# One chain of squares per half, and attention heads placed between projection chunks

## The reference, cut to what matters

```python
# x: (16, 2048, 1024); 4 heads of 256; 256 memory tokens
x = x + merged @ w_out[l]                      # mixer's output projection
hq = rms_norm(x, xattn_norm_g[l])
q = (hq @ w_q[l]).reshape(b, s, 4, 256)
k, v = jnp.split(mem_n @ w_kv[l], 2, axis=-1)
pr = softmax(einsum("bshd,bmhd->bhsm", q, k) * 256 ** -0.5)
x = x + einsum("bhsm,bmhd->bshd", pr, v).reshape(b, s, d) @ w_o[l]
hf = rms_norm(x, ffn_norm_g[l])
...
x = x + (gelu(gate) * val) @ w_down[l]         # gated MLP
# rms_norm(x, g) = x * rsqrt(mean(x*x) + 1e-6) * g
```

## Time and profile before

| | |
|---|---|
| runs | 4116.72 us median of 3 (4114.6 to 4533.86) |
| profiled execution | 4116.1 us; span of its slowest core 4114.6 us, of the others 4102.6 to 4113.3 us |
| PE busy | 3876.9 us (94%), 18224 matmuls |
| DVE busy | 2683.5 us (65%) |
| ACT busy | 1953.7 us (47%) |
| POOL busy | 197.7 us (5%) |
| mean granted TensorE clock | 0.984 to 0.988 by core |
| chain that ended last | PE 81%, ACT 7%, DVE 6%, issue 3%, DMA 2% |

### The profile page before, as it was taken

How to read it: one execution, slowest core, us unless ns; L and a number is a source line. 1 busy time by engine, 2 the same in 40 slices (tenths; PEclk the granted TensorE clock), 3 DMA queues, 4 the chain that set the end, 5 groups by cost and what they waited for, 6 DMA issues and landing times.

```text
span 4114.6 us, 56669 instructions; the slowest of 8 cores (4102.6 to 4114.6 us)
## 1 busy us (share of the span) xinstructions
PE 3876.9 (94%) x18224; PEld 1784.1 (43%) x18224; DVE 2683.5 (65%) x3336; ACT 1953.7 (47%) x3779; POOL 197.7 (5%) x379
## 2 busy tenths in 40 slices
PE   6999999999998999999989999999999999999998
PEld 3444444444443445434444444543444434444343
DVE  4538775387754876649675387653867549665587
ACT  3445444464444544446443464434644346452544
POOL 1000000000000000000010000000000000000000
PEclk9999999999999999999999999999999999999999
DMA  6443352434842345323464424534346424352342
GB/s 138 117 82 68 65 107 58 82 68 80 168 103 51 59 78 110 62 49 67 106 136 103 84 56 81 99 64 84 65 108 136 103 49 73 68 106 52 57 75 70
DMA packets 108815, 348.19 MB, mean 85 GB/s; under 512 B 11888, under 2 KB 46960, under 8 KB 83952
## 3 DMA queue, kind: packets, MB, share of 16 engines
q0 software_dynamic: 41760, 275.11, 37.0%
q1 hardware_dynamic: 66768, 69.46, 5.7%
HBM read 586.05 MB, written 16.78 MB: 147 GB/s over the span
## 4 chain that ended last, share of the span: by engine, by line
PE 81%; ACT 7%; DVE 6%; issue 3%; DMA 2%; SPq 0%; DVEq 0%; ACTq 0%; POOLq 0%; POOL 0%
PE ps L424 81%; DVE X L401 2%; ACT SQ L397 2%; DVE H L411 2%; ACT F L397 2%; ACT AR L397 2%; DMA AR<-AR 1%; DVE SQ L401 1%; DVE X L411 1%; ACT RS L397 0%; DMA AR<-xT 0%; SPq L872 0%; ACT L397 0%; DVE F L411 0%; DMA RING<-wst 0%
## 5 line engine op out<-in xcount | busy, mean ns | idle before, releaser
L424 PE MATMUL ps<-H,RING 128*128 128x512 bf16 x10240 | 2265.0, 381 | 66.4 <-ACT GB L397 25.3
L424 PEld LDWEIGHTS ps<-H,RING 128*128 128x128 bf16 x10240 | 1004.2, 98 | 1286.6 <-issue 110.7
L424 PE MATMUL ps<-AR,RING 128*128 128x512 bf16 x4864 | 1096.7, 386 | 0.0
L397 ACT ACTIVATE AR<-ps 128x512 bf16<-128x512 f32 (+1 forms) x1024 | 598.5, 600 | 637.8 <-PE ps L424 610.8
L411 DVE SCALAR_TENSOR_TENSOR F<-AR,VEC,F 128x1024 f32<-128x1024 bf16 (+1 forms) x576 | 687.9, 1194 | 111.8 <-ACT F L397 69.1
L424 PEld LDWEIGHTS ps<-AR,RING 128*128 128x128 bf16 x4864 | 482.7, 99 | 590.2 <-issue 39.1
L397 ACT ACTIVATE SQ<-X 128x512 bf16<-128x512 f32 x384 | 240.2, 629 | 599.8 <-DVE X L401 561.9
L401 DVE TENSOR_TENSOR X<-ps,X 128x512 f32<-128x512 f32 x512 | 339.6, 684 | 200.3 <-PE ps L424 200.2
L397 ACT ACTIVATE GB<-ps 128x512 bf16<-128x512 f32 x320 | 183.1, 604 | 433.1 <-PE ps L424 431.5
L397 ACT ACTIVATE GB<-F 128x1024 bf16<-128x1024 f32 x192 | 189.3, 986 | 287.0 <-DVE F L411 286.4
L515 POOL DMA_DIRECT2D RING<-wst x280 | 147.8, 528 | 3598.7 <-PE ps L424 3578.4
(11 more groups left out here) (75 smaller groups left out, 1954.5 us busy)
## 6 DMA issues: line engine op xcount, KB each, us to landing
RING<-wst POOLq DMA_DIRECT2D x184, 1024.0 KB, 9.3
RING<-wst POOLq DMA_DIRECT2D x64, 704.0 KB, 7.8
RING<-wst POOLq DMA_DIRECT2D x32, 768.0 KB, 6.7
AR<-AR SPq DMA_DIRECT2D x256, 64.0 KB, 3.5
X<-xT SPq DMA_DIRECT2D x64, 256.0 KB, 12.8
yT<-X SPq DMA_DIRECT2D x64, 256.0 KB, 9.4
AR<-xT SPq DMA_DIRECT2D x40, 256.0 KB, 7.0
WX<-wst POOLq DMA_DIRECT2D x8, 1280.0 KB, 15.9
```

What stands on the lines that cost most here:

```text
L397: S.add("act", lambda h: h.activation(out=out.ap, in_=in_.ap, func=func, scale=s, **kw), reads=rd, writes=out.keys)
L424: S.add("pe", lambda h: h.matmul(out.ap, lhsT=lhsT.ap, rhs=rhs.ap, start=start, stop=stop), reads=lhsT.keys + rhs.keys, writes=out.keys)
```

## The change

`residual_stage` is split: `residual_items` gives the list of chunks, and the stage runs them as before. In it the squares of a half form one chain, with each addition issued one chunk after its square was, and one ONESK matmul after chunk 7. `proj_group` gives its inner loop to `run_items`. `attn` now projects Q for s = 0 first; then it runs heads 0 to 2 of s = 0, with Q chunks of s = 1 between a head's scores and its denominator; then head 3 of s = 0 and head 0 of s = 1 as a pair; then heads 1 to 3 of s = 1, with output chunks of s = 0 between. The output projection's `lead_group` is gone.

```diff
--- before.py
+++ after.py
@@ -647,14 +647,17 @@
                     flush()
                 if lead[s]:
                     lead_group(items[:lead[s]], s)
-                for blk, ncol, col0, rhs, evac in items[lead[s]:]:
-                    b_ = blk(s) if callable(blk) else blk
-                    nk = len(rhs)
-                    ps = P.next()
-                    for kc in range(nk):
-                        MM(ps.v(), b_.v(kc * ncol + col0, kc * ncol + col0 + 128), sub(rhs[kc], s), kc == 0, kc == nk - 1)
-                    evac(s, ps)
-                    tick()
+                run_items(items[lead[s]:], s)
+
+        def run_items(items, s):
+            for blk, ncol, col0, rhs, evac in items:
+                b_ = blk(s) if callable(blk) else blk
+                nk = len(rhs)
+                ps = P.next()
+                for kc in range(nk):
+                    MM(ps.v(), b_.v(kc * ncol + col0, kc * ncol + col0 + 128), sub(rhs[kc], s), kc == 0, kc == nk - 1)
+                evac(s, ps)
+                tick()
 
         def norm_stats_fin(s, pn):
             rs = RSB.v(s * ST, (s + 1) * ST)
@@ -673,33 +676,40 @@
                     reads=o.keys, dma_sem="out%d_%d" % (c, s))
                 out_tokens.append(tok)
 
-        def residual_stage(items_wo_evac, kind, gbase, lead):
+        def residual_items(items_wo_evac, kind, gbase):
             pn = [P.take(), P.take()]
             last = kind == "final"
             lag_apply = (3, 5) if last else (0, 0)
             b, hf = now["b"], now["hf"]
 
-            prev_sq = {}
+            sqs = [[], []]
 
             def mk(oc):
                 def ev(s, ps):
                     TT("dve", sub(X[oc], s), ps.v(), sub(X[oc], s), ALU.add)
                     sq = SQR.next()
                     ACT(sq.v(), sub(X[oc], s), AF.Square)
-                    if oc % 4:
-                        TT("dve", sq.v(), sq.v(), prev_sq[s].v(), ALU.add)
-                    prev_sq[s] = sq
+                    sqs[s].append(sq)
+
+                    def add():
+                        a, b_ = sqs[s].pop(0), sqs[s][0]
+                        TT("dve", b_.v(), b_.v(), a.v(), ALU.add)
+
+                    if oc >= 2:
+                        add()
                     tag = 2 if last else s
-                    if oc % 4 == 3:
-                        defer(lambda: MM(pn[s].v(), ONESK.v(), sq.v(), oc == 3, oc == 7), 3, tag)
                     if oc == 7:
+                        add()
+                        defer(lambda: MM(pn[s].v(), ONESK.v(), sq.v(), True, True), 3, tag)
                         defer(lambda: norm_stats_fin(s, pn), 3, tag)
                         for c in range(8):
                             defer(lambda c=c: norm_apply(s, c, kind, gbase, b, hf), 3 + lag_apply[s] + c // 2, tag)
                 return ev
 
-            items = [(blk, ncol, col0, rhs, mk(oc)) for oc, (blk, ncol, col0, rhs) in enumerate(items_wo_evac)]
-            proj_group(items, True, (lead, 0))
+            return [(blk, ncol, col0, rhs, mk(oc)) for oc, (blk, ncol, col0, rhs) in enumerate(items_wo_evac)]
+
+        def residual_stage(items_wo_evac, kind, gbase, lead):
+            proj_group(residual_items(items_wo_evac, kind, gbase), True, (lead, 0))
 
         def mem_load(b):
             for i_ in range(2):
@@ -975,33 +985,56 @@
                         ACT(VV[mc].v(jb * 512, (jb + 1) * 512), ps.v(), AF.Copy)
                         tick()
             wqb = [ring_get(l, "wq0"), ring_get(l, "wq1")]
-            proj_group([(wqb[qc // 4], 512, (qc % 4) * 128, H,
-                         (lambda s, ps, qc=qc: ACT(sub(Q[qc], s), ps.v(), AF.Identity, scale=1.0 / 16))) for qc in range(8)], True, (0, 4))
-            ri = 0
-            for hd in range(4):
-                for s in range(2):
-                    E = []
+            qi = [(wqb[qc // 4], 512, (qc % 4) * 128, H,
+                   (lambda s, ps, qc=qc: ACT(sub(Q[qc], s), ps.v(), AF.Identity, scale=1.0 / 16))) for qc in range(8)]
+            expd = {}
+
+            def scores(hd, s):
+                expd[hd, s] = []
+                for mc in range(2):
+                    ps = P.next()
+                    for dc in range(2):
+                        MM(ps.v(), KT[2 * hd + dc].v(mc * 128, (mc + 1) * 128), sub(Q[2 * hd + dc], s), dc == 0, dc == 1)
+                    e = EBR.next()
+                    ACT(e.v(), ps.v(), AF.Exp)
+                    expd[hd, s].append(e)
+
+            def heads(hd, s):
+                E = expd.pop((hd, s))
+                psd = P.next()
+                for mc in range(2):
+                    MM(psd.v(), ONES1.v(), E[mc].v(), mc == 0, mc == 1)
+                rd = F[(2 * hd + s) % 4]
+                ACT(rd.v(0, ST), psd.v(), AF.Ln)
+                ACT(rd.v(0, ST), rd.v(0, ST), AF.Exp, scale=-1.0)
+                for dc in range(2):
+                    pso = P.next()
                     for mc in range(2):
-                        ps = P.next()
-                        for dc in range(2):
-                            MM(ps.v(), KT[2 * hd + dc].v(mc * 128, (mc + 1) * 128), sub(Q[2 * hd + dc], s), dc == 0, dc == 1)
-                        e = EBR.next()
-                        ACT(e.v(), ps.v(), AF.Exp)
-                        E.append(e)
-                    psd = P.next()
-                    for mc in range(2):
-                        MM(psd.v(), ONES1.v(), E[mc].v(), mc == 0, mc == 1)
-                    rd = F[ri % 4]
-                    ri += 1
-                    ACT(rd.v(0, ST), psd.v(), AF.Ln)
-                    ACT(rd.v(0, ST), rd.v(0, ST), AF.Exp, scale=-1.0)
-                    for dc in range(2):
-                        pso = P.next()
-                        for mc in range(2):
-                            MM(pso.v(), VV[mc].v(hd * 256 + dc * 128, hd * 256 + (dc + 1) * 128), E[mc].v(), mc == 0, mc == 1)
-                        TT("dve", sub(ATT[2 * hd + dc], s), pso.v(), rd.v(0, ST), ALU.mult)
+                        MM(pso.v(), VV[mc].v(hd * 256 + dc * 128, hd * 256 + (dc + 1) * 128), E[mc].v(), mc == 0, mc == 1)
+                    TT("dve", sub(ATT[2 * hd + dc], s), pso.v(), rd.v(0, ST), ALU.mult)
+
+            flush_tag((0,))
+            run_items(qi, 0)
+            flush()
+            for hd in range(3):
+                scores(hd, 0)
+                if hd == 0:
+                    lead_group(qi[0:4], 1)
+                else:
+                    run_items(qi[2 * hd + 2:2 * hd + 4], 1)
+                heads(hd, 0)
+            scores(3, 0)
+            scores(0, 1)
+            heads(3, 0)
+            heads(0, 1)
             wab = [ring_get(l, "woa0"), ring_get(l, "woa1")]
-            residual_stage([(wab[oc // 4], 512, (oc % 4) * 128, ATT) for oc in range(8)], "H", LB + 72, 3)
+            oi = residual_items([(wab[oc // 4], 512, (oc % 4) * 128, ATT) for oc in range(8)], "H", LB + 72)
+            for hd in range(1, 4):
+                scores(hd, 1)
+                run_items(oi[2 * hd - 2:2 * hd], 0)
+                heads(hd, 1)
+            run_items(oi[6:8], 0)
+            run_items(oi, 1)
 
         def ffn(l, hf):
             LB = l * NVL
```

## The result

The change is faster: the ratio of its time to that of the kernel before is 0.9645, with a 95% interval of 0.9617 to 0.9673, where the forecast of 3963 us was 0.963. Three runs took 3967.83, 3969.14 and 3971.54 us. Run again later, beside three other versions, the change took 3963.99 to 3972.18 us, ratio 0.9613 (0.9571 to 0.9656).

The account below looks back on a forecast made before the run. PE, busy for 94% of the span, bounds the kernel. 22.4 + 1.7 + 30.6 + 28.5 + 9.3 + 11.0 + 1.7 + 51.0 - 3 = 153.2 us, off 4116.1, gives 3963 us; range 3920 to 4012 us.

Parts of the forecast that it names:

- Ahead of T: Stretch before T: 22.4 us gained in mixer and attention stages, 1.7 us in the MLP's, where only a matmul goes.
- T: Start of the first half's ONESK matmul, which stands after chunk 1 of the second half before and after the change.
- From T to the second sum: From T to the second half's ONESK, the wait moves: gains 30.6 us mixers, 28.5 attention, 9.3 and 11.0 MLP layers.
- the last stage: The very last MLP stage, which has no H products for a next unit: 1.7 us, by the removed wait alone.
- rival B: The late sum stays late because the first half's H products set it: 81 us lost, 4044 us; chance 0.05.
- Rival C: Waits go altogether if ACT delivers RS 1.5 to 3 us earlier than read: 3924 us; chance 0.06.
- Heads: Attention's heads: 80 matmuls at 17.26 us instead of 24.04, less 0.4 us at the pair; gain 51.0 us.
- The rival that ACT covers only half: In attention's heads PE still waits behind ACT's queue, or banks run out: half of 51, 3989 us; chance 0.09.
- Clock: Waits of about 3 us left in mixer stages may lower the clock: nothing to 13.5 us, 3 us taken.
- a sign of failure: Prediction fails if attention's granted clock falls, the first H starts after T + 4.9, or bank waits appear on PE.
- The rival of a denser PE with a slower clock: Denser PE is granted less, from second-half Q through output projection: 470 us lost, 4433 us; chance 0.02.
- so the ring is not squeezed: In attention, weight blocks are asked for in the old order and Q blocks' last reader comes earlier; no size given.

Follow-up runs that it names:

- the paired heads: The change without projection chunks between heads: both halves of Q first, each head's scores ahead of the head before; 3970.41 to 3978.98 us, ratio 0.964.
- without the stores: The change without the stores of the result for the first three of the four units; 3946.94 and 3949.53 us, ratio 0.9577.
- the stores late: The change with a unit's result stores issued after the next unit's transfers to the convolution's layout; 3947.86 to 3952.21 us, ratio 0.9564.
- the one that gained nothing: The change with one sum per half but each square added promptly, as before; median 4125.3 us, ratio 1.0026.
- the heads alone: The change's placed heads, with squares added promptly and two sums per half as in the kernel before; 4067.45 us, a single run.
- the squares alone: The change's new chain of squares, with attention as in the kernel before; 4019.94 to 4026.79 us, ratio 0.9762.

## Where the prediction was right and which step failed, point by point

**Ahead of T.** 22.4 us for mixers and attention: 18.66 us became 17.27, so 1.39 us each. Right.

**From T to the second sum.** Mixers 30.6 us forecast, 33.1 measured (166.63 less 133.49), since the first H came at T + 4.51 and not at T + 4.86. That was a misreading of one stage as the rule: in the kernel before, too, the first H comes at T + 4.51 in six of the eight mixers, and the stage that I read is one of the other two. ACT is not earlier: its second RS starts at T + 3.78 in that stage (1242.94) and in the change (1206.48). In the kernel before, at the mixer whose T is 206.72, DVE's timeline has:

```profile
211.23 1.41 DVE L411 SCALAR_TENSOR_TENSOR H<-X,VEC,RS 128x512 bf16<-128x512 f32 x2 [2.29 <-ACT RS L397]
```

Attention 28.5 and 28.1 (150.45 less 122.39), layer-0 MLPs 9.3 and 9.2, layer-1 MLPs 11.0 and 10.9, the last stage 1.7 and 1.7 (sum at T + 16.9). The wait moved rather than vanished, and in mixers and attention DVE's chain from the first H on sets its size. So rival B, that the sum stays late, falls. Rival C, that the waits go, falls too: 1.74 to 2.46 us are left per mixer.

**Heads.** 51.0 us forecast with 0.4 us left at the pair; 0.65 us was left, so 49.0. The rival that ACT covers only half falls: its queue had the slack that the count of operations gave.

**Clock.** I took 3 us, between 0 and 13.5. In the windows from T to the second sum it was 0. Behind the second sum it was not: four mixers have keys and values behind them and a wait of 2.46 us at the sum, and after it the 32 matmuls on MEMN took 3.49 us twice and 5.16 us twice (from start to the next group's start), with a granted clock of 0.50 in the middle of that stretch. The first of each kind (start, us, what):

```profile
226.07 3.65 PE L424 MATMUL ps<-MEMN,RING 128*128 128x256 bf16 x32
...
714.22 5.32 PE L424 MATMUL ps<-MEMN,RING 128*128 128x256 bf16 x32
```

That is 2 x 1.67 = 3.3 us. So the term was right in size, but it was a guess between two ends, and that it hit is luck. It also is what I had named as a sign of failure, a granted clock that falls in attention, twice and for some 3 us each. The rival of a denser PE with a slower clock falls: PE at 96% has a mean clock of 0.991 to 0.993, above the 0.984 to 0.988 before. Of the pace, the Trainium skill's 131 ns (TensorE: Matmul & The Clock Gate, section "Back-to-back issue gap") stays contradicted: 80 matmuls in 17.27 us are 0.216 us each, and so are the 80 of the paired heads in 17.30.

**The sum, and the step that failed.** The terms as measured give 22.4 + 1.7 + 33.1 + 28.1 + 9.2 + 10.9 + 1.7 + 49.0 = 156.1 us. The spans differ by 144.6, 11.5 us less. The stretches from one stage's second sum to the next stage's T show where it went. The four that begin a unit lose 13.4 us against the terms: 3.9 at the kernel's start, 9.5 at the three other units. The clock takes 3.3. The other stretches give about 5.4 us more than the terms, which I cannot name one by one.

At the kernel's start the first weight load and what hangs on it came later on the profiled core (the group of matmuls at 64.83 us starts at 68.85). Over the cores this load's waits are 8.1 to 12.9 us before, 11.2 to 16.8 after, and 5.3 to 15.6 when the change was run again. The change touches nothing there, so I take it for chance.

The step that failed is in the paragraph on the heads: "so the ring is not squeezed". It looked only at the weight ring, and the sum put every other transfer at nothing. The runs showed longer waits of PE for the transfers to the convolution's layout at the three unit starts: 2.63, 5.38 and 1.27 us before, 4.79, 5.38 and 6.30 after, 7.2 us more. It is not one core's chance: the mean over the eight cores of the three waits together is 8.3 us before, 15.3 after and 16.7 when the change was run again. The stores are needed for them, since without the stores the mean is 0.5 us and with the stores late 0.8. That they grow when units end sooner fits the other versions (5.7 us over four cores of the one that gained nothing, 12.9 with the heads alone, 16.4 over four cores with the squares alone). What then meets what is not shown: the DMA engines' busy share is 0.89 in the last window above and was 0.93 in the same one before. The sum's own answer, 3963, was 5 to 9 us too low, with 7.2 us missing for the transfers.

## What to carry to other kernels

When an engine in the middle of a loop must add up what another engine has just made from its own result, issue the addition one step later: the wait is not on the bottleneck's list of work, but it comes out there. Before removing a wait, write down the in-order chain of the engine that causes it, with pitches from the trace; it tells not only that the wait goes but what remains and where, to some tenths of a microsecond here. Read such a chain from several stages of the same kind, since one of them can be the exception. And ask of each stage that ends sooner which transfers now meet.

## What the runs showed of the hardware that I had not expected

A DMA issue costs ACT's queue 0.63 us each (four in 2.51 us) for transfers of 64 KB, which is more than one 512-column activation (0.60 us). Stores issued first hold up small transfers issued after them: 13.40 us to landing at a unit's start. With the stores issued later, the change gained some 20 us (3948 to 3952 against 3964 to 3972). And the clock: the same wait in the same place is followed by 1.2 GHz or not. In the change, the group of 32 matmuls behind the second sum of the four mixers with keys and values is shown at 3.65 or 3.66 us in 19 of 32 cases over the eight cores and at 4.93 to 5.32 us in 13. In the kernel before, an attention's window with one wait of 2.52 us was at 0.91 in seven of eight cases and at 1.00 in the eighth. So a wait of about 2.5 us can cost 1.7 us more behind it, and one profiled core does not tell how often.
